# Input projection of a decoder block: eight chunks of 452 columns or seven of 516, each product's columns in one PSUM bank or in two

## What is computed

```python
h = rms_norm(x, norm_mix)                      # (256, 2048)
y = h @ w_in                                   # w_in: (2048, 9752)
(qa, ka, va, qb, kb, vb, qc, kc, vc, ksl, vsl, kwn, vwn, gc, gates) = split_cols(y, IN_SPLITS)
y_a = swa_attention(...)                       # from qa, ka, va
y_b = stick_breaking(...)                      # from qb, kb, vb
y_c = nsa_attention(...)                       # from qc .. vwn, gc
merged = sigmoid(g_a) * (y_a @ w_br_a) + sigmoid(g_b) * (y_b @ w_br_b) + sigmoid(g_c) * (y_c @ w_br_c)
x = x + merged @ w_out
x = x + (silu(rms_norm(x) @ w_gate) * (rms_norm(x) @ w_up)) @ w_down
out = rms_norm(x)
```

## Time and profile before

| | us |
|---|---|
| median of 3 runs | 1384.41 |
| lowest and highest | 1384.26, 1385.81 |
| span of the profiled execution | 1378.3 |
| TensorE busy | 1364.8 (99%) |
| VectorE busy | 922.5 (67%) |
| ScalarE busy | 702.5 (51%) |

### The profile page before, as it was taken

How to read it: one execution, slowest core, us unless ns; L and a number is a source line. 1 busy time by engine, 2 the same in 40 slices (tenths; PEclk the granted TensorE clock), 3 DMA queues, 4 the chain that set the end, 5 groups by cost and what they waited for, 6 DMA issues and landing times.

```text
span 1378.3 us, 26427 instructions
## 1 busy us (share of the span) xinstructions
PE 1364.8 (99%) x11280; PEld 1332.1 (97%) x11280; DVE 922.5 (67%) x1189; ACT 702.5 (51%) x912; POOL 46.2 (3%) x70
## 2 busy tenths in 40 slices
PE   8999999999999999999999999999999999999997
PEld 8999999999999999999999999999999999999997
DVE  6455557667654657666788788875446788887554
ACT  7333356656545654465654555454334455545444
POOL 4000010000000110000000000000000000000111
PEclk9999999999999999999999999999999999999999
DMA  7777755455565767546556756566556665666653
GB/s 255 245 217 217 212 148 154 140 151 141 152 192 163 198 204 221 179 163 200 165 181 198 219 171 196 185 208 210 195 195 181 191 211 172 196 194 231 210 195 123
DMA packets 135264, 261.08 MB, mean 189 GB/s; under 512 B 8448, under 2 KB 25408, under 8 KB 134768
## 3 DMA queue, kind: packets, MB, share of 16 engines
q1 hardware_dynamic: 133328, 251.89, 59.8%
q0 software_dynamic: 1792, 7.57, 1.5%
q10 hardware_dynamic: 32, 0.01, 0.0%
HBM read 257.33 MB, written 2.10 MB: 188 GB/s over the span
## 4 chain that ended last, share of the span: by engine, by line
PE 89%; DVE 8%; ACT 1%; issue 1%; ACTq 0%; POOL 0%; DVEq 0%; POOLq 0%
PE bank L638 24%; PE bank L639 23%; PE bank L640 23%; PE bank L877 5%; PE bank L880 4%; PE bank L879 4%; PE bank L627 2%; DVE weight_lo_ring L1269 2%; DVE weight_sums_lo L1289 1%; DVE weight_sums L1278 1%; PE bank L776 1%; DVE act_rows L1329 1%; ACT weight_hi_ring L1039 1%; PE bank L687 1%; DVE raw_ring L1280 1%
## 5 line engine op out<-in xcount | busy, mean ns | idle before, releaser
L1269 DVE TENSOR_TENSOR weight_lo_ring<-raw_ring,weight_hi_ring 128x1024 fp32r<-128x1024 f32 (+2 forms) x480 | 581.0, 1220 | 317.0 <-ACT weight_hi_ring L1039 263.4
L1039 ACT ACTIVATE weight_hi_ring<-raw_ring 128x1024 fp32r<-128x1024 f32 (+2 forms) x432 | 449.1, 1052 | 348.6 <-PE bank L640 281.1
L638 PE MATMUL bank<-weight_hi_ring,hT_hi 128*128 128x256 f32 (+2 forms) x1280 | 384.5, 300 | 0.8 <-DVE weight_lo_ring L1269 0.8
L639 PE MATMUL bank<-weight_lo_ring,hT_hi 128*128 128x256 f32 (+2 forms) x1280 | 378.0, 295 | 0.0
L640 PE MATMUL bank<-weight_hi_ring,hT_lo 128*128 128x256 f32 (+2 forms) x1280 | 377.8, 295 | 0.0
L638 PEld LDWEIGHTS bank<-weight_hi_ring,hT_hi 128*128 128x128 f32 x1280 | 241.1, 188 | 12.5 <-issue 7.5
L639 PEld LDWEIGHTS bank<-weight_lo_ring,hT_hi 128*128 128x128 f32 x1280 | 240.5, 188 | 4.5
L640 PEld LDWEIGHTS bank<-weight_hi_ring,hT_lo 128*128 128x128 f32 x1280 | 240.4, 188 | 4.7
L638 PE MATMUL bank<-weight_hi_ring,h2T_hi 128*128 128x256 f32 x704 | 196.3, 279 | 2.2 <-DVE weight_lo_ring L1269 2.1
L640 PE MATMUL bank<-weight_hi_ring,h2T_lo 128*128 128x256 f32 x704 | 195.3, 277 | 0.0
L639 PE MATMUL bank<-weight_lo_ring,h2T_hi 128*128 128x256 f32 x704 | 195.2, 277 | 0.0
(11 more groups left out here) (238 smaller groups left out, 1883.2 us busy)
## 6 DMA issues: line engine op xcount, KB each, us to landing
raw_ring<-in_w_in SPq DMA_DIRECT2D x96, 512.0 KB, 3.6
raw_ring<-in_w_gate SPq DMA_DIRECT2D x88, 512.0 KB, 4.3
raw_ring<-in_w_up SPq DMA_DIRECT2D x88, 512.0 KB, 4.2
raw_ring<-in_w_down SPq DMA_DIRECT2D x88, 512.0 KB, 4.1
raw_ring<-in_w_in SPq DMA_DIRECT2D x56, 452.0 KB, 3.7
raw_ring<-in_w_out SPq DMA_DIRECT2D x32, 512.0 KB, 3.9
raw_ring<-in_w_br_c SPq DMA_DIRECT2D x16, 256.0 KB, 3.9
raw_ring<-in_w_br_a SPq DMA_DIRECT2D x16, 256.0 KB, 6.7
```

The lines of the kernel that those rows point to most:

```text
L638: pe.matmul(dst, x_hi, w_hi, start=opening, stop=False, skip_group_check=True)
L639: pe.matmul(dst, x_hi, w_lo, start=False, stop=False, skip_group_check=True)
L1039: act.activation(whi[:, s, :, 0:width(u)], raw[:, s, :, 0:width(u)], ACT.Copy).then_inc(hi_ready, 1)
L1269: dve.tensor_tensor(lo, w, hi.bitcast(F32), ALU.subtract).then_inc(lo_ready, 1)
```

## The change

The projection gets seven chunks of 516 columns (six of 516 and one of 512), which is 56 units in place of 64. A unit's blocks are cut in halves of `HQ = 258` columns (254 in the last chunk's second half); each half of each token tile has a PSUM bank of its own, four banks a chunk (`four_of`: 4 to 7 for even chunks, 0 to 3 for odd ones), and a unit is 2 x 2 x 2 x 3 = 24 products.

A slot of `raw` grows from 1024 to 1032 numbers. A slot of `whi` and `wlo` grows to four pieces of `STEP_Q = 320` numbers, each holding one half of a block. So the moving operand begins 128 bytes into a 512-byte line for first halves, and 384 bytes into one for second halves. The later stages use the first 1024 numbers of a slot, as before.

Chunk 0 has banks 4 to 7 now, so the transposes of x go to banks 0 to 3, the first gains to bank 3, the other three to bank 0 and after unit 6. TensorE waits for ScalarE's copy of these (`gains_ready`) ahead of chunk 1. The waits for `squares`, which kept bank 3 from being overwritten, are gone; the junk of the squares goes to `proj`. `dynamic_dma_scratch_size=8192` makes room in SBUF. The loop has two rounds, and two chunks are written out behind it.

```diff
-WQ = 452
+WQ = 516
+HQ = WQ // 2
+STEP_Q = 320
...
+def pair_of(q):
+
+    return (q - N_QKV) % 2
+
+
+def four_of(q):
+
+    return 4 * ((q + 1) % 2)
...
-        raw = place("raw_ring", [RING, UK, W])
-        whi = place("weight_hi_ring", [RING, UK, W], F32R)
-        wlo = place("weight_lo_ring", [RING, UK, W], F32R)
+        raw_slots = place("raw_ring", [RING, UK * WQ])
+        top[0] += (MOVING - top[0]) % LINE
+        hi_slots = place("weight_hi_ring", [RING, 4 * STEP_Q], F32R)
+        lo_slots = place("weight_lo_ring", [RING, 4 * STEP_Q], F32R)
...
+        hi_halves, lo_halves = (m[:, :, :].rearrange("p s (g n) -> p s g n", g=4) for m in (hi_slots, lo_slots))
...
+            def products_q(slot, four, first, last, k0, width=WQ):
+
+                for k, t, h in [(k, t, h) for k in range(UK) for t in range(TT) for h in range(2)]:
+                    n = min(HQ, width - h * HQ)
+                    dst = bank[four + 2 * t + h][:, 0:n]
+                    x_hi, x_lo = (m[:, k0 + k, t * P:(t + 1) * P] for m in (hT_hi, hT_lo))
+                    w_hi, w_lo = (m[:, slot, 2 * k + h, 0:n] for m in (hi_halves, lo_halves))
+                    pe.matmul(dst, x_hi, w_hi, start=first and k == 0, stop=False)
+                    pe.matmul(dst, x_hi, w_lo, start=False, stop=False)
+                    m = pe.matmul(dst, x_lo, w_hi, start=False, stop=last and k == UK - 1)
+                return m
...
-                if u == 3:
+                if u == 6:
                     pe.wait_ge(rows_ready, 48)
-                    pe.wait_ge(gains_ready, 1)
                     for a in range(1, 4):
-                        m = transpose(bank[2][:, KD * a:KD * (a + 1)], rows[0:KD, a, :], KD)
+                        m = transpose(bank[0][:, KD * a:KD * (a + 1)], rows[0:KD, a, :], KD)
                     m.then_inc(gains_full, 1)
+            pe.wait_ge(gains_ready, 2)
...
-                        products(u0 % RING, (hT_hi, hT_lo), q0 % 2, j == 0, j == UPC - 1,
-                                 UK * j, WQ).then_inc(unit_used, 1)
-            for u in range(U_MIX - UPC, U_FFN):
+                        products_q(u0 % RING, four_of(q0), j == 0, j == UPC - 1, UK * j).then_inc(unit_used, 1)
+            for u in range(U_MIX - 2 * UPC, U_FFN):
...
+                act.activation(hi_halves[:, s, :, 0:HQ], raw_halves[:, s, :, :], ACT.Copy).then_inc(hi_ready, 1)
...
+                dve.tensor_tensor(lo_halves[:, slot, :, 0:HQ], raw_halves[:, slot, :, :],
+                                  hi_halves[:, slot, :, 0:HQ].bitcast(F32), ALU.subtract).then_inc(lo_ready, 1)
...
+            def empty_projection(q, cols_of):
                 for t in range(TT):
-                    last = dve.tensor_scalar(proj[:, t, cols], bank[2 * pair + t][:, 0:w], rstd[:, t:t + 1], None, ALU.mult)
+                    for h in range(2):
+                        cols, w = cols_of(h)
+                        last = dve.tensor_scalar(proj[:, t, cols], bank[four_of(q) + 2 * t + h][:, 0:w], rstd[:, t:t + 1],
+                                                 None, ALU.mult)
```

More of the change, by code:

```diff
@@ L352, in build_layer @@
         s_w = pT[:, 1, 0, :]
-        bank = [ctx.enter_context(nc.psum_tensor(f"bank{i}", [P, W], F32)) for i in range(8)]
+        banks = ctx.enter_context(nc.psum_tensor("banks", [P, 8, W], F32))
+        bank = [banks[:, i, :] for i in range(8)]
         def sem(name):
@@ L659, in straight @@
                     pair_free(q)
-                    if q == 1:
-                        pe.wait_ge(squares, 2 * NC_D)
+                if kind == "qkv":
+                    if q == 0:
+                        pe.wait_ge(t_lo, j + 1)
+                    unit_q(u, q, j, width(u))
+                    return
                 if kind == "branch":
@@ L1119, in follow @@
                     for t in range(TT):
-                        last = act.activation(sig[:, i % SIG, t, :], bank[2 * (q % 2) + t][:, :], ACT.Sigmoid,
+                        last = act.activation(sig[:, i % SIG, t, :], bank[2 * pair_of(q) + t][:, :], ACT.Sigmoid,
                                               scale=rstd[:, t:t + 1])
@@ L1219, in gains @@
                 act.wait_ge(gains_full, n)
-                src = bank[2][:, KD * a.start:KD * a.stop].rearrange("p (a k) -> p a k", k=KD)
+                src = bank[3 if n == 1 else 0][:, KD * a.start:KD * a.stop].rearrange("p (a k) -> p a k", k=KD)
                 act.activation(gainT[:, a, :], src, ACT.Copy).then_inc(gains_ready, 1)
@@ L1232, in _ @@
                     act.wait_ge(x_ready[n // 2 + 1], 16)
-                    square(n % 2, n // 2, bank[3], n)
-                if m == 5:
-                    gains(2, slice(1, 4))
+                    square(n % 2, n // 2, proj[:, TT - 1, 0:W], n)
+            gains(2, slice(1, 4))
             root(1)
@@ L1238, in _ @@
                 for j in range(2 * UPC):
-                    split_in_loop(UPC + j, i * (2 * UPC // RING), i * (2 * UPC), WQ)
-            for u in range(U_MIX - UPC, U_END + LAG):
+                    split_in_loop(UPC + j, i * (2 * UPC // RING), i * (2 * UPC))
+            for u in range(U_MIX - 2 * UPC, U_END + LAG):
                 if u < U_END:
@@ L1289, in split @@
                     dve.tensor_tensor(ext_lo[:, e, :, :], t_sum[:, :, :], ext_hi[:, e, :, :].bitcast(F32), ALU.subtract)
-                split_unit(u % RING, u + 1, width(u))
+                if u < U_MIX:
+                    split_halves(u % RING, u + 1)
+                else:
+                    split_unit(u % RING, u + 1)
                 if is_seven(u + 1) and is_seven(u):
@@ L1408, in follow @@
                 kind, i, _, n = CHUNKS[q]
-                pair = q % 2
+                pair = pair_of(q)
                 if j == n - 1 and kind == "qkv":
                     dve.wait_ge(unit_used, v + 1)
-                    empty_projection(pair, slice(i * WQ, min((i + 1) * WQ, N_PROJ)), width(v))
+                    empty_projection(q, half_columns(q))
                 if j == n - 1 and kind == "branch":
```

69 lines of the change are left out of this document (42 added, 27 removed).

## The result

The changed kernel is slower: 1393.12 us (1389.0 to 1398.3, 6 runs) against 1383.37 us (1380.39 to 1385.81, 6 runs), ratio 1.0064 with an interval of 1.0038 to 1.0089. (The ratios in this document are the record's own estimates with 95% intervals, and not quotients of the two medians; that quotient would be 1.0070 here.) The forecast was 1379.7 us and its range ended at 1389 us.

What follows compares the result with a forecast made beforehand. It took the projection as bound by a gapless row of TensorE products. Products -5.1, start +0.25 and pause +0.1 gave -4.75 us, so 1384.4 became 1379.7 us; the 8-in-10 range was 1375.5 to 1389 us.

Steps and rivals of the forecast that it cites:

- The products: Projection on TensorE: 1344 narrower products at 114.2 or 112.5 ns take 153.3 us in place of 158.4, 5.1 us less.
- The point of equal cost: Projection: at 117.6 ns a product, the changed kernel would take as long as the one before.
- Rival 1: Projection products: fixed part plus a rate slightly under a column a clock, 118.9 ns at 258 columns; 1386.0 us; chance 0.27.
- Rival 2: Projection products: excess belongs to each weight load under the columns, with shifted addresses; 125.9 ns, 1395.4 us; chance 0.13.
- Rival 3: Projection products: separate banks for the halves leave nearly no excess, 110 ns; 1374.2 us; chance 0.06.
- Rival 4: Projection: a unit's splits or transfer come late, so products are traded for waits; chance 0.04 together with the rest.
- TensorE's new wait for the gains: End of unit 7: ScalarE's 0.2 us copy of the gains is covered by the 2.7 us unit; cost nothing.
- The pause: After unit 6: the three small gain rows' transposes make a pause of their own, breaking the product row; +0.1 us.
- Start: First product: larger ScalarE and VectorE splits delay it by 0.25 us, 0.2 us more if the first weights land late.
- the splits: ScalarE's high part and VectorE's low part of a unit's weights: 1068 and 1230 ns for 1032 numbers.
- the emptying: End of a chunk: four VectorE instructions of 258 columns take some 1.8 us, 0.5 us more, fitting into 1.36 us.
- The transfers: Weights for the projection: 516 KB a unit in 2.74 us, 193 GB/s, covered by the products.

Runs made afterwards that it cites:

- experiment 1: Changed kernel with second halves 384 numbers behind the first, with 256-column products, and with both: 1392.59, 1378.82, 1384.47 us, beside 1383.17 for the kernel before.

## Why the prediction was wrong

**The products: this is the term that failed.** "I take the excess of the nearest width, 256, in its usual rhythm: 107.5 + 6.7 = 114.2 ns." The distance was 120.8 ns, an excess of 13.3: 1344 products make +4.0 us in place of -5.1, 9.1 of the 13.4 us by which the forecast missed. The bounds, 107.5 and 125.9 ns, held it; the choice between them took a neighbour two columns away as the same thing. The 112.5 ns for 254 columns failed alike: the last chunk, half of it 254 wide, has 120.0 ns a product. The rows ahead of the prediction had something that speaks against this: 452, 444 and 256 lie on no one line through the columns, and 256 was the only width whose excess was small. A width that stands out among those measured is no evidence for the one beside it. The 203 ns for 444 columns was read over six products; over the whole chunk it is 202.2, which changes 0.1 us. The point of equal cost, 117.6 ns, was worked out rightly.

**Rival 1** (118.9 ns, 1386.0 us) was the nearest by its price and right in its sign, but its line of rate and fixed part is refuted by 264 columns, which cost as much as 258. **Rival 2** (weight loads against shifted addresses, 125.9 ns, 1395.4 us) came nearest to the measured 1393.1 us, and by luck, for experiment 1 shows its reason to be wrong: 256 columns with the same loads and shifted addresses take 113.3 ns. **Rival 3** fell: 256 columns with banks of their own take as long as with shared ones. **Rival 4**, waits in place of products, holds in one place.

**TensorE's new wait for the gains: "nothing".** Here the step itself was wrong. It asked whether ScalarE's copy would be ready for TensorE, and it was. It did not ask what is queued behind the copy on ScalarE: the root, whose result VectorE waits for with the low part of unit 8 behind it. 1.4 us. The pause, which had been priced at +0.1, cost nothing.

**Start.** +0.25 for the larger splits, and 0.2 more if the weights land late: the first product was 0.44 us later in this trace, so both together: ScalarE began the first high part at 6.67 in place of 6.51 us. In the second trace it began at 6.50, and the first product was 0.29 us later. The half clock behind it, 0.9 us, was in no term; it comes with either kernel, and the trace that the sum was made on was one of the two without it.

**Right:** the splits, 1068 and 1230 ns; the forms view of the changed kernel (mean in ns behind the busy time):

```profile
L1315 DVE TENSOR_TENSOR weight_lo_ring<-raw_ring,weight_hi_ring 128x1032 fp32r<-128x1032 f32 x56 | 68.8, 1232 | 60.9 <-ACT weight_hi_ring L1081 60.1 <-DVE rstd L1443 0.2
L1081 ACT ACTIVATE weight_hi_ring<-raw_ring 128x1032 fp32r<-128x1032 f32 x56 | 59.5, 1067 | 80.6 <-PE banks L671 76.2 <-DMA raw_ring<-in_w_in 4.3
```

and the emptying, some 1.8 us forecast for four of 258 columns, and covered:

```profile
177.17 1.66 DVE L1454 TENSOR_SCALAR proj<-banks,rstd 128x258 f32<-128x258 f32 x4 [0.56 <-PE banks L671]
...
179.80 0.69 PE L762 MATMUL banks<-identity,proj 128*64 128x64 f32 x16
```

It ends at 178.83 us, the first mixer transposes need it at 179.80 us, and have no wait. The transfers are covered too: no wait on one inside the projection. The prediction's own test named the outcome: "I am wrong if ... its 258-column products come at over 117.6 ns."

## What to carry to other kernels

Where a kernel is a gapless row of products, its time is a count times a distance, and the distance has to be measured at the very width that is planned: two columns more cost 6% here, the next six nothing, and eight fewer cost 3%. If work is moved to a later place, follow the queue behind the instruction that waits for it, on every engine in turn, until somebody is reached who is on the path; the wait itself may be harmless and the one behind it not. Look at the distance of the first products to see which clock they had, and whether the traces compared began alike; dummy products that fill an idle start went with a full clock in the one trace here, no more. Price a stage by several executions before a difference of 2 us is explained.

## What the runs showed of the hardware

- The distance between fp32r products of 128 rows, each with its own weight load, does not grow evenly with their columns: 116.7 ns at 248, 113.3 at 256, 120.0 at 258 and 264, 166.7 at 360, 206.7 at 452, 213.3 at 464, 216.0 at 480. The rule of the Trainium skill that the prediction weighed ("TensorE: Matmul & The Clock Gate", Back-to-back issue gap: columns at 2.4 GHz and about 2.5 ns) gives 110.0 ns at 258, 10.8 less than was measured. That section gives the formula for a product in isolation, and says that in a stream of weight loads and products both set the distance. The products here are such a stream, so the formula that the prediction weighed was not meant for them.
- One width can have two rhythms that hold for tens of us: 113.3 and 117.8 ns at 256 columns, 120.0 and 120.8 at 258. How long each holds differs between traces; in the 16 traces of the study the same later work took from 1198.8 to 1207.0 us.
- Second halves that begin 256 bytes further in a 512-byte line cost nothing: 113.3 ns at 256 columns either way, and both 120.0 and 120.8 ns occur at 258 columns with either address.
- TensorE ran at 1.2 GHz at the start of every trace (transposes of 128 columns 213 ns apart from 1.87 us on). The first record of the full clock came at 5.0 to 6.6 us in eight of the 16 traces, and at 10.0 to 13.6 us in the other eight; in six of the first eight it was 0.50 again from 8.4 to 9.2 us until 11.9 to 15.2 us. The same kernel had both starts: the kernel before rose at 5.8 us in one trace and at 10.6 us in the other. TensorE waited 0.7 to 2.1 us for x in 15 traces, and not at all in the filled one.
